# Prompt attention: the turns of probabilities given as rounded 32-bit values over the same bytes

## What is computed

```python
l_s = jnp.einsum('bqgrd,bgqkld->bgrqkl', q, k_sel).astype(jnp.float32)
l_s = l_s.reshape(b, g, r, nq, n_sel * SLC_BLOCK) * scale + bias_s
p_s = masked_softmax(l_s, m_s)
o_s = jnp.einsum('bgrqn,bgqnd->bqgrd', p_s.astype(v_sel.dtype),
                 v_sel.reshape(b, g, nq, n_sel * SLC_BLOCK, dh))
...
o = gates[..., 0:1] * o_c + gates[..., 1:2] * o_s + gates[..., 2:3] * o_w
```

## Time and profile before

| | us |
|---|---|
| time, median of 3 runs | 2966.76 |
| lowest and highest run | 2964.34, 2969.48 |
| span of the profiled execution | 2966.2 |
| TensorE products, busy in the span | 2784.7 |
| VectorE, busy in the span | 1854.9 |
| ScalarE, busy in the span | 1227.5 |
| GpSimd, busy in the span | 1219.1 |
| first turn of the stage, from the span's start | 434.0 |
| last product by values, from the span's start | 793.2 |

### The profile page before, as it was taken

One profiled execution on the slowest core, in us unless ns is written; L12 is line 12 of the kernel. 1 busy time (PEld: TensorE's weight loads), 2 busy tenths in 40 slices (PEclk: granted clock), 3 DMA queues, 4 the chain that ended last, 5 costly groups with the idle time before them and its releaser, 6 DMA issues. The chain is left out here.

```text
span 2966.2 us, 54771 instructions
## 1 busy us (share of the span) xinstructions
PE 2784.7 (94%) x21032; PEld 2557.0 (86%) x21032; DVE 1854.9 (63%) x3420; ACT 1227.5 (41%) x2492; POOL 1219.1 (41%) x788
## 2 busy tenths in 40 slices
PE   8998979999989998999999789899998999998898
PEld 8996966666767798899999789888898999998798
DVE  6212148888545526777777666695348777877665
ACT  5002027777633414454545333314335455444332
POOL 3440000000000144555555788660336555457786
PEclk9999989999989999999999899999999999999999
DMA  6216750000257320222223222313111222222322
GB/s 189 57 42 233 228 178 21 2 2 2 96 168 227 122 102 24 84 70 84 70 84 106 94 93 73 117 60 119 36 49 48 84 74 84 78 104 80 120 82 86
DMA packets 168199, 272.16 MB, mean 92 GB/s; under 512 B 19702, under 2 KB 112220, under 8 KB 166768
## 3 DMA queue, kind: packets, MB, share of 16 engines
q1 hardware_dynamic: 141636, 225.19, 23.0%
q10 hardware_dynamic: 26316, 43.66, 4.5%
HBM read 226.22 MB, written 46.69 MB: 92 GB/s over the span
## 5 line engine op out<-in xcount | busy, mean ns | idle before, releaser
L3122 PE MATMUL banks<-token_blocks_high,weight_blocks_high 128*128 128x272 f32 x3584 | 753.4, 292 | 78.1 <-POOL weight_blocks_low L3009 29.1
L3122 PE MATMUL banks<-token_blocks_low,weight_blocks_high 128*128 128x272 f32 x3584 | 745.2, 290 | 0.0
L3122 PE MATMUL banks<-token_blocks_high,weight_blocks_low 128*128 128x272 f32 x3584 | 744.6, 290 | 0.0
L3122 PEld LDWEIGHTS banks<-token_blocks_high,weight_blocks_high 128*128 128x128 f32 x3584 | 565.6, 191 | 88.5 <-issue 54.2
L3122 PEld LDWEIGHTS banks<-token_blocks_low,weight_blocks_high 128*128 128x128 f32 x3584 | 569.4, 191 | 0.0
L3122 PEld LDWEIGHTS banks<-token_blocks_high,weight_blocks_low 128*128 128x128 f32 x3584 | 566.4, 191 | 0.0
L3009 POOL TENSOR_TENSOR weight_blocks_low<-ight_quarters_more,weight_blocks_high 128x512 fp32r<-128x512 f32 (+2 forms) x150 | 221.5, 1478 | 173.3 <-ACT weight_blocks_high L3146 173.0
L3402 DVE SCALAR_TENSOR_TENSOR conv_space<-conv_space,conv_w 128x1024 f32<-128x1024 f32 x176 | 238.3, 1354 | 73.7 <-ACT conv_space L3201 62.2
L3009 POOL TENSOR_TENSOR weight_blocks_low<-weights_whole,weight_blocks_high 128x512 fp32r<-128x512 f32 (+2 forms) x146 | 220.1, 1509 | 139.5 <-ACT weight_blocks_high L3146 139.2
L3009 POOL TENSOR_TENSOR weight_blocks_low<-weights_again_whole,weight_blocks_high 128x512 fp32r<-128x512 f32 (+2 forms) x146 | 212.1, 1455 | 140.6 <-ACT weight_blocks_high L3146 138.6
L3440 DVE TENSOR_TENSOR x<-x,banks 128x544 f32<-128x544 f32 x224 | 160.4, 718 | 152.4 <-PE banks L3122 148.4
(11 more groups left out here) (514 smaller groups left out, 5523.8 us busy)
## 6 DMA issues: line engine op xcount, KB each, us to landing
gated_scratch<-conv_space ACTq DMA_DIRECT2D x44, 544.0 KB, 3.7
past_rows<-in_kv_pages SPq DMA_DIRECT2D x160, 128.0 KB, 2.4
ight_quarters_more<-in_w_up SPq DMA_DIRECT2D x56, 256.0 KB, 2.9
weights_whole<-in_w_up SPq DMA_DIRECT2D x56, 256.0 KB, 3.1
weights_again_whole<-in_w_up SPq DMA_DIRECT2D x56, 256.0 KB, 2.9
staged<-gated_scratch SPq DMA_DIRECT2D x16, 816.0 KB, 6.5
z<-in_kv_pages SPq DMA_DIRECT2D x96, 128.0 KB, 2.4
x<-in_cmp_pages ACTq DMA_DIRECT2D x64, 128.0 KB, 5.4
```

The source lines that it names most:

```text
L3122: last = pe.matmul(out[:, piece, :], a[:, at], b[:, kk, piece * HP:(piece + 1) * HP], start=first and kk == 0 and z == 0, stop=kk == n - 1 ...
```

## The change

For each of the tiles of probabilities, a second tensor of the type F32R is declared at the same address (`moved_by_bits`), and for the third large unit one over `z`. `to_turn` picks among them as `selected` and `window` do among the plain ones. The turns at L1353 read these, with an identity of the type F32R (`ident_r`), and write the bank under the same type; ScalarE still reads the bank as F32. The identity is copied once by VectorE at the head of the stage. Nothing else is changed: the order, the semaphores and the counts of TensorE's instructions stay. Unlike the other rounded tiles of this kernel, the probabilities are not written by an instruction that rounds them.

```diff
+        def moved_by_bits(name, t):
+            return nc.alloc_sbuf_tensor_at(name + "_to_turn", list(t.shape), F32R, offset=k.at[t.name])
+
+        turn_sel_small, turn_win_small, turn_sel_large, turn_win_large, turn_lc = (
+            moved_by_bits(name, t) for name, t in (("selected_small", sel_small), ("window_small", win_small), ("selected_large", sel_large),
+                                                   ("window_large", win_large), ("blocks", lc)))
+        turn_third_sel, turn_third_win = thirds(moved_by_bits("z", z))
+        ident_r = k.sb(ctx, "ident_rounded", [P, P], F32R)
...
+        def to_turn(u, what):
+
+            s = u // 2 % RING
+            if what == "c":
+                return turn_lc[:, slot(u), :, :]
+            if u % 2 == 0:
+                return (turn_sel_small if what == "s" else turn_win_small)[:, s, :, :]
+            if s < RING - 1:
+                return (turn_sel_large if what == "s" else turn_win_large)[:, s, :, :]
+            return turn_third_sel if what == "s" else turn_third_win
...
-                    src, w = {"s": (selected(u), P), "w": (window(u), P), "c": (lc[:, slot(u), :, :], NCP)}[what]
+                    src, w = to_turn(u, what), NCP if what == "c" else P
                     for g in range(G):
                         at_col = (2 * y + g) * P
-                        last = pe.transpose(turned_bank(a)[0:w, at_col:at_col + P], src[:, g, col:col + w], c["ident"][:, :])
+                        last = pe.transpose(turned_bank(a)[0:w, at_col:at_col + P].bitcast(F32R), src[:, g, col:col + w], ident_r[:, :])
                 last.then_inc(turned, 1)
...
             dve.memset(mx[:], LOWEST)
+            dve.tensor_copy(ident_r[:, :], c["ident"][:, :])
             dve.drain()
```

## The result

| us | before | after |
|---|---|---|
| time, median of six runs each | 2969.09 | 2954.03 |
| lowest and highest run | 2964.34, 2975.07 | 2950.88, 2961.75 |
| span of the profiled execution | 2966.2 | 2950.4 |
| first turn of the stage, from the span's start | 434.0 | 434.0 |
| last product by values, from the span's start | 793.2 | 776.5 |

The ratio is 0.9946 with a 95% interval of 0.9933 to 0.996: 16.0 us faster, between 11.9 and 19.9. In after, the turn has moved from L1353 to L1376, the values from L1369 to L1392, the scores from L1332 and L1337 to L1355 and L1360, ScalarE's copy from L1549 to L1573.

What follows compares the result with a forecast made beforehand. TensorE was taken to pace the prompt attention's middle. 14.6 us there plus 3.4 at its end made 18.0 us, so 2966.8 - 18.0 = 2948.8 us; its own range was 2932 to 2961, with 8 in 10 for 2932 to 2971.

Steps and rivals of the forecast that it cites:

- What bounds the stage: Prompt attention, 460 to 750 us: TensorE busy for all 290.00 us paces it; three starts in four wait for no other engine.
- What a turn costs: Each of 888 plain turns: 0.109 us, set by the moved identity at two cycles a column, not by the load.
- The rounded turn: Changed turns: 82 ns each, the middle between 0.057 and 0.109 us, from a quicker stream with a partly uncovered load.
- the first rival: Turns: nothing changes, the rounded turn streams as before or its load takes the pace at 0.11 us; 2966.8 us, chance 0.33.
- The sum: 27 ns saved a turn: three quarters of the middle's 19.5 us, 14.6, plus 3.4 at the end, 18.0 us in all.
- the first 40-odd turns: Stage's head, where the pipeline fills: no gain counted.
- The forecast's cap: Middle stretch: VectorE can give up 22.0 us of waits for scores, then paces the stage at some 235 us.
- The third rival: Turns at the full stream, 57 ns, 34.7 us saved: 2932 us, counted in as the forecast's lower end, no chance of its own.
- The second: Rival, middle and end: the rounded load is no longer hidden, 848 x 0.057 = 48 us slower, 3015 us; chance 0.12.
- The small parts: Stage's head: VectorE's identity copy takes 0.28 us ahead of a 1.75 us wait, so costs nothing, 0.3 us without that wait.
- The signs named: Profile after: four turns in about 0.52 us, loads of 141 or 191 ns, closer block turns if load-set, clock 1.00.
- The sign by grown waits ahead of loads: If pace falls but time doesn't, waits of TensorE's loads on ScalarE's copies and VectorE's maxima must have grown as much.

Runs made afterwards that it cites:

- the further plain turn: Kernel before with each of the 888 plain turns issued twice into the same place: 3063.44 us, ratio 1.0324.
- lighter helpers: Kernel before, ScalarE taking exponentials of and VectorE scaling only half of the tiles' columns, turns reading that half again: 2966.44 us, ratio 0.9988.
- once ScalarE was light: Changed kernel with ScalarE alone taking exponentials of only half of each row's tiles, VectorE scaling all: 2944.88 us, ratio 0.9921.
- half of the identity: Only 64 queries of a tile turned, 64 identity columns moved: 2940.0 us on the kernel before, 2941.43 us on the changed kernel.
- the plain copy: Kernel before with the identity copied by VectorE into its own tile of the plain type, turns staying plain: 2971.52 us, ratio 1.0005.
- rounded turns in memory and samples together: Changed kernel with the turns of the memory attention and of the sample attention rounded as well: ratio 0.9979, executions 2948.42 to 2999.38 us.
- the rounded kernel with light helpers: Changed kernel, ScalarE taking exponentials of and VectorE scaling only half of the tiles' columns, turns reading that half again: 2937.92 us, ratio 0.9899.

## Why the prediction was right, and where its steps were not

The forecast was 2948.8 us, the time 2954.03 against 2969.09 measured beside it; a gain of 18.0 us was worked out and 16.0 came. Sign, size and place hold. Two terms behind the 18.0 were off, in opposite directions, and two reasons were wrong: that of the share and that of the rounded turn's pace.

**What bounds the stage.** Held, and more sharply than I put it: the further plain turn cost 0.108 us each with nothing to absorb it, and lighter helpers gave 3.6 us, 1.1 of them behind the stage's head. The forecast's reading of 77 of 313 waits on helpers as a quarter of TensorE's time that can't be won was wrong for the kernel before. A helper that ends a wait isn't one that sets the pace.

**What a turn costs.** The plain pace of 109 ns and its cause, the moved identity at two cycles a column, held: with 64 columns the pace fell to 0.062 us.

**The rounded turn.** 82 ns were taken, 86 measured, but not as "a quicker stream with a load that is partly uncovered". The stream did get faster, to 62 ns or less (62 forecast), and then the load took the pace. That is the mechanism of the first rival at a smaller price: its load would take 0.11 us, by the ordinary loads of the earlier trace rows; the turns' take 0.085. The sign that was named for it told it apart: block turns closer than full ones. The Trainium skill, "TensorE: Matmul & The Clock Gate", section LDWEIGHTS (loading the stationary operand), gives columns / 1.2 ns, an estimate of 107 ns for 128 columns whatever the partitions. The ordinary loads' 0.11 us agree, the rounded turns' 0.085 and the plain turns' 0.062 don't, and that 64 partitions took 0.085 as 128 did agrees. The Trainium skill, "TensorE: Matmul & The Clock Gate", section Back-to-back issue gap, has some 81 ns for one of a stream of pairs of load and 128-column product, set by both. The rounded turns' 86 ns agree within 5, the plain turns' 109 don't.

**The sum.** The step that failed in size is the saving per turn: 27 ns forecast, 23 by the pace, 28 by whole stretches, since the pace has no term for the first distance and the tail of each of the 120 stretches, nor for the block turns (25.4 - 888 x 0.023 = 5.0 us). The other is the share that reaches the time: 0.75 of the middle, and nothing from the first 40-odd turns, were forecast, and 16.0 / 25.4 = 0.63 of all came. The share was drawn from a list of waits that the light helpers show to have cost next to nothing; that it came out near (17.5 of 23.9 us, 0.73, from the first to the last turn of `z`) is luck. That the first turns give nothing was near too: the head lost some 3 us against what they are worth, for a reason that stays open. The forecast's cap, VectorE's spare waits and a pace of 235 us, was the wrong reason as well. VectorE gave up half of its waits for scores, but it went to 240.40 of 275 us and held nothing back once ScalarE was light. What held the saving back were short waits that lighter exponentials on ScalarE, which the cap did not count, remove.

**The third rival** could not have had its price: with the load at 0.085 us a turn at 57 ns wasn't to be had, and with half of the identity, which frees TensorE for 14 to 20 us of the middle, the time was still 2940 us, not 2932. **The second** is out: the pace fell.

**The small parts.** The copy took 0.16 us (0.28 forecast) ahead of a wait that shrank from 1.75 to 1.67; its place and its cost were right, and the plain copy's time says so alone.

**The signs named.** Four turns at the head of a stretch last 0.54 us (the row at 774.43 above), where the forecast had 0.52 for four inside one; the loads last 140 ns, not 191; the clock is 1.00 in the middle. These went the way of the forecast, the block turns the way of the first rival. The sign by grown waits ahead of loads was a poor one, as light helpers left them as long.

What stays open: why a rounded load is slower, what slows the stage's head, why rounded turns in memory and samples together did not give what they gave apart, and whether three turned banks instead of two would give back the loss to the helpers, which wasn't tried.

## What to carry to other kernels

A turn had two paces here, that of its load and that of its moved columns, and the slower counted; look at a form with a short load, for it tells which of the two rules. A saving on the engine that paces a stage is first worth its full price. What the other engines hold back of it showed neither in how often they end a wait nor in how full they are: VectorE at 87% held nothing back once ScalarE, at 80%, was lightened. Make the helpers lighter and the engine heavier, one at a time, and compare the same stretch of work in the traces: it repeated within 0.2 us here, where the whole time moved by several.

## What the runs showed of the hardware

- A 32-bit turn of 128 columns goes every 0.109 us in the plain type and every 0.086 in the rounded one; the type alone does it.
- The plain turn is bound by its moved identity, the rounded one by its load, 0.085 us against at most 0.062 for the plain load, with 64 partitions as with 128. The record of a load, 0.14 us, doesn't show it.
- In the rounded kernel with light helpers the idle time ahead of loads that a helper ended, 29.3 us in a stretch of 275 (19.5 + 5.5 + 4.3), cost nothing, as the products stayed busy.
